# Mixture-of-experts stage of a two-layer decoder: two-pass products for experts with up to 64 tokens, experts ordered on the chip, wide splits in the weight ring, layer loop unrolled

## The reference

```python
def swiglu(h, w1, w3, w2):
    return (jax.nn.silu(h @ w1) * (h @ w3)) @ w2

def moe_swiglu(h, router, w1, w3, w2):
    logits = (h @ router).astype(F32)
    top_v, top_i = lax.top_k(logits, TOP_K)
    gates = jax.nn.softmax(top_v, axis=-1)
    dense_gate = jnp.sum(jax.nn.one_hot(top_i, N_EXPERTS, dtype=F32) * gates[..., None], axis=-2)
    y = jnp.zeros(h.shape, F32)
    for e in range(N_EXPERTS):
        y = y + swiglu(h, w1[e], w3[e], w2[e]).astype(F32) * dense_gate[..., e:e + 1]
    return y.astype(h.dtype)
```

## Time and profile before

| | |
|---|---|
| Median of 3 runs | 1658.33 us (1656.91 to 1659.19) |
| Profiled execution, its own time | 1656.95 us |
| Its span, first to last instruction | 1655.3 us |
| PE busy | 1579.4 us, 95% |
| DVE busy | 1181.1 us, 71% |
| ACT busy | 1001.2 us, 60% |
| Mean granted TensorE clock | 0.977 |
| DMA | 433.46 MB, mean 262 GB/s |
| of it expert weights | 168 DMAs of 2 MB |
| Chain that ended last | PE 90%, DVE 3%, ACT 3%, issue 2%, DMA 1% |

### The profile page before, as it was taken

One profiled execution on the slowest core, in us unless ns is written; L12 is line 12 of the kernel. 1 busy time (PEld: TensorE's weight loads), 2 busy tenths in 40 slices (PEclk: granted clock), 3 DMA queues, 4 the chain that ended last, 5 costly groups with the idle time before them and its releaser, 6 DMA issues.

```text
span 1655.3 us, 21928 instructions
## 1 busy us (share of the span) xinstructions
PE 1579.4 (95%) x7746; PEld 1288.8 (78%) x7746; DVE 1181.1 (71%) x1486; ACT 1001.2 (60%) x1182; POOL 51.8 (3%) x64
## 2 busy tenths in 40 slices
PE   5999989999799978999999999999999999999997
PEld 4776679998676556888888888888888888888885
DVE  1514255555244237998998998998998998998996
ACT  2322254433223134887887887887887887887885
POOL 0230000000032000000000000000000000000000
PEclk9999999999799997999999999999999999999999
DMA  8523415542722182999999999999999999999970
GB/s 297 180 77 126 166 38 193 197 146 61 269 76 77 63 319 102 354 371 339 355 370 334 356 371 331 355 372 331 357 369 333 355 367 335 357 373 329 356 291 25
DMA packets 190711, 433.46 MB, mean 262 GB/s; under 512 B 5679, under 2 KB 30277, under 8 KB 190661
## 3 DMA queue, kind: packets, MB, share of 16 engines
q1 hardware_dynamic: 190468, 432.24, 72.4%
q0 software_dynamic: 192, 0.53, 0.1%
HBM read 431.70 MB, written 1.05 MB: 261 GB/s over the span
## 4 chain that ended last, share of the span: by engine, by line
PE 90%; DVE 3%; ACT 3%; issue 2%; DMA 1%; SPq 0%; ACTq 0%; DVEq 0%; PEldq 0%
PE bank L1216 65%; PE bank L1193 7%; PE bank L1198 5%; PE bank L1474 3%; PE bank L1564 2%; PE bank L1183 2%; PE bank L1615 1%; PE bank L1514 1%; PE bank L1369 1%; DVE w_lo L1150 1%; ACT w_hi L722 1%; PE bank L1581 0%; ACT xg_hi L688 0%; PE bank L1582 0%; ACT r L639 0%
## 5 line engine op out<-in xcount | busy, mean ns | idle before, releaser
L1150 DVE TENSOR_TENSOR w_lo<-ring,w_hi 128x1024 fp32r<-128x1024 f32 x672 | 804.8, 1223 | 90.2 <-ACT w_hi L722 64.9
L722 ACT ACTIVATE w_hi<-ring 128x1024 fp32r<-128x1024 f32 x672 | 709.5, 1062 | 192.0 <-PE bank L1216 188.4
L1216 PE MATMUL bank<-w_hi,xg_hi 128*128 128x512 f32 x896 | 357.3, 399 | 6.9 <-DVE w_lo L1150 6.8
L1216 PE MATMUL bank<-w_lo,xg_hi 128*128 128x512 f32 x896 | 350.4, 391 | 0.0
L1216 PE MATMUL bank<-w_hi,xg_lo 128*128 128x512 f32 x896 | 349.7, 390 | 0.0
L1216 PEld LDWEIGHTS bank<-w_hi,xg_hi 128*128 128x128 f32 x896 | 168.5, 188 | 50.0 <-DVE w_lo L1150 16.7
L1216 PEld LDWEIGHTS bank<-w_lo,xg_hi 128*128 128x128 f32 x896 | 168.5, 188 | 36.6
L1216 PEld LDWEIGHTS bank<-w_hi,xg_lo 128*128 128x128 f32 x896 | 168.9, 188 | 32.6
L1216 PE MATMUL bank<-w_hi,at_hi 128*128 128x512 f32 x448 | 175.9, 393 | 0.0
L1216 PE MATMUL bank<-w_lo,at_hi 128*128 128x512 f32 x448 | 174.5, 389 | 0.0
L1216 PE MATMUL bank<-w_hi,at_lo 128*128 128x512 f32 x448 | 174.4, 389 | 0.0
(11 more groups left out here) (298 smaller groups left out, 1591.4 us busy)
## 6 DMA issues: line engine op xcount, KB each, us to landing
ring<-in_moe_w SPq DMA_DIRECT2D x168, 2048.0 KB, 7.9
ring<-in_ffn_w SPq DMA_DIRECT2D x18, 1536.0 KB, 6.7
ring<-in_w_in SPq DMA_DIRECT2D x6, 2048.0 KB, 14.7
ring<-in_w_out SPq DMA_DIRECT2D x8, 1024.0 KB, 4.9
ring<-in_ffn_w SPq DMA_DIRECT2D x3, 2048.0 KB, 7.8
ring<-in_w_in SPq DMA_DIRECT2D x4, 1024.0 KB, 16.4
ring<-in_xa_wkv SPq DMA_DIRECT2D x2, 2048.0 KB, 12.5
ring<-in_w_in SPq DMA_DIRECT2D x2, 1184.0 KB, 5.6
```

Of the source, the lines that this page charges most:

```text
L722: act.activation(w_hi[:, i % NB, :], ring[:, slot_of(u), PIECE * q:PIECE * q + PIECE], ACT.Copy)\
L1150: dve.tensor_tensor(w_lo[:, i % NB, :], ring[:, slot_of(u), PIECE * q:PIECE * q + PIECE], w_hi[:, i % NB, :], sub).then_inc(S["lo_ready"], 1)
L1216: ins = mm(dst, x, y, start=opens and n % 3 == 0, stop=closes and n % 3 == 2)
```

## The change

**Jobs ordered on the chip.** The table of jobs is built differently. For expert e, a full job is made if its count is above a limit, -1 for expert 0 and 64 for the others (the table `limit`), a second full job if it is above 128, and a small job otherwise. Full jobs come first, then the small ones. The table now also holds each job's expert (SP reads it for every job after the first), the number of full jobs, and a third row of token positions, in which a small job's are shifted by 64. The mask of job 0 is made before the table.

**Small jobs.** The mask of a small job has its up to 64 tokens twice, in columns 0 to 63 and 64 to 127. So `xg_both`, the 128 columns from 64 to 191 of `xg`, is the hi of the tokens beside their lo, and two products, with w_lo and w_hi, do what three did: the rows 0 to 63 of the bank hold hi·(w_hi + w_lo), rows 64 to 127 lo·(w_hi + w_lo). ACT copies both banks out as they are, PE adds the two halves while it transposes them (`fold`, 8 plain float32 matmuls of 64 columns), ACT makes Silu of 256 elements, DVE the product, its hi and its lo side by side in `at_hi`. Both kinds of jobs have a loop of their own on PE, ACT and DVE.

**Wide pieces in place.** A piece is 2048 columns, but for units (1,0) and (3,0), which are cut into 1024, 1024 and 2048: 44 pieces a job. `w_hi` has 4 buffers of 2048. There is no `w_lo` any more: DVE writes it over the weights in the ring slot (`ring_lo`), and PE gives the slot back at the last but one matmul of the unit. `after(unit)` is the unit's last piece plus 3 (`LEAD`). The dense feed-forward keeps pieces of 1024.

**Layers unrolled.** The loop over the two layers is written out on all engines, `If` blocks are decided at build time, and waits are on constants.

```diff
-PIECE, NB = 1024, 4
-QP = 4096 // PIECE
+PIECE, NB = 2048, 4
+FPIECE = 1024
+SMALL = 64
+LEAD = 3
+CUTS = [(u, *cut) for u in range(len(JOB_UNITS))
+        for cut in (((0, 1024), (1024, 2048), (2048, 4096)) if u < 2 else ((0, 2048), (2048, 4096)))]
+LAST = {u: i for i, (u, _, _) in enumerate(CUTS)}
 def after(unit):
-    return QP * UNIT_OF[unit] + QP - 1 + NB
+    return LAST[UNIT_OF[unit]] + LEAD
+    put("limit", np.concatenate(([-1.0], np.full(N_EXP - 1, SMALL), np.full(N_EXP, P)))[None, :])
...
-        w_hi, w_lo = over("w_hi", [P, NB, PIECE]), over("w_lo", [P, NB, PIECE])
-        xg_hi, xg_lo = over("xg_hi", [P, KT, P]), over("xg_lo", [P, KT, P])
+        w_hi = over("w_hi", [P, NB, PIECE])
+        xg = over("xg", [P, KT, 2 * P])
+        xg_hi, xg_lo = xg[:, :, 0:P], xg[:, :, P:2 * P]
+        fold = diag[:, 0, 0:SMALL]
+        xg_both = xg[:, :, SMALL:SMALL + P]
...
-            with sp.Fori(0, DEPTH) as layer:
+            for layer in range(DEPTH):
...
-            with sp.Fori(0, N_EXP) as j:
-                job_loads(j, j)
+            job_loads(0, 0)
             sp.wait_ge(S["jobs_ready"], 1)
...
+            with sp.Fori(1, n_jobs) as j:
+                e = sp.value_load(tabi[0:1, bass.ds(j + 2, 1)], min_val=0, max_val=N_EXP - 1)
+                job_loads(j, e)
```

ACT's pieces (`first_rows` waits for `j_h1` and makes Silu, or a plain copy in a small job; `small_silu` waits for `j_tps`):

```diff
                 for i in range(JOB_PIECES):
-                    if i in (NB - 1, NB):
-                        yrow_out(j, i - (NB - 1))
+                    if i == NB - 1:
+                        for half in range(2):
+                            yrow_out(j, half)
                     for c in range(NCH):
+                        last = i == JOB_PIECES - 1 if c == NCH - 1 else i == after((1, c + 1)) + 1
+                        if not small and i == after((1, c)):
+                            first_rows(c)
+                        if last and small:
+                            small_silu(c)
+                        elif last:
                             transposed(cn[c])
+                        if small and i == after((1, c)) + 1:
+                            first_rows(c)
+                        if small and i == after((3, c)):
+                            act.wait_ge(S["j_h3"], cn[c])
+                            act.activation(s_rows[1], ps[2 * (c % 2) + 1][:, :], ACT.Copy).then_inc(S["j_a"], 1)
```

DVE:

```diff
+                def small_act(c):
+                    dve.wait_ge(S["j_s"], cn[c])
+                    dve.tensor_tensor(s_act, v3(s_sil, 0, 256, 4), v3(ps[4], 256, 512, 4), mult).then_inc(S["j_m"], 1)
+                    dve.wait_ge(S["j_m"], cn[c])
+                    dve.tensor_copy(at_hi[:, :, 0:SMALL], s_act).then_inc(S["j_th"], 1)
+                    dve.wait_ge(S["j_th"], cn[c])
+                    dve.tensor_tensor(at_hi[:, :, SMALL:P], s_act, at_hi[:, :, 0:SMALL], sub).then_inc(S["j_t"], 1)
...
-                    dve.tensor_tensor(w_lo[:, i % NB, :], ring[:, slot_of(u), PIECE * q:PIECE * q + PIECE],
-                                      w_hi[:, i % NB, :], sub).then_inc(S["lo_ready"], 1)
+                    dve.tensor_tensor(ring_lo[slot_of(u)][:, cols], ring[:, slot_of(u), cols],
+                                      w_hi[:, i % NB, 0:cols.stop - cols.start], sub).then_inc(S["lo_ready"], 1)
+            with dve.Fori(0, n_full) as j:
+                job(j, False)
+            with dve.Fori(n_full, n_jobs) as j:
+                job(j, True)
```

PE:

```diff
+                            steps.append((dst[:, :], xh, wh, opens, False))
+                            if small:
+                                steps.insert(len(steps) - 1, (dst[:, :], xh, wl, opens, False))
+                                steps[-1] = (dst[:, :], xh, wh, False, closes)
+                            else:
+                                steps += [(dst[:, :], xh, wl, False, False), (dst[:, :], xl, wh, False, closes)]
+                        for x, (dst, st_, mv, opens, closes) in enumerate(steps):
+                            ins = mm(dst, st_, mv, start=opens, stop=closes, skip_group_check=small)
+                            if x == 0:
+                                ins.then_inc(S["piece_free"], 1)
+                            elif i == LAST[u] and x == len(steps) - 2:
+                                ins.then_inc(slot_free[slot_of(u)], 1)
...
+                    if small:
+                        for x in range(2):
+                            for f in range(4):
+                                i = mm(ps[4][:, 256 * x + SMALL * f:256 * x + SMALL * f + SMALL],
+                                       s_rows[x][:, P * f:P * f + P], fold, start=True, stop=True)
```

## The result

| | kernel before | kernel after |
|---|---|---|
| median of the runs | 1658.76 us (1656.91 to 1659.44) | **1574.15 us** (1573.18 to 1575.1, 4 runs) |
| ratio, 95% interval | | 0.9492 [0.9475, 0.9508] |
| profiled span, granted clock | 1655.3 us | 1571.5 us, 0.975 |

The kernel is 84.6 us faster, 5.1%. 1585 was predicted, with 1558 to 1628 as the range. The medians of the kernel before, measured beside the experiments, lie between 1655.6 and 1657.7 us.

What follows compares the result with a forecast made beforehand. PE was taken to bound the expert stage, with DMA and DVE close behind. Six small jobs -70.4, two full jobs +5.2, unrolled layers -8.3 and the job table +0.5 make -73.0 us: 1585 us, range 1558 to 1628.

Steps and rivals of the forecast that it cites:

- The limit of a small job: Each small job: DVE's work of 107.8 us plus waits of 1.5 and 3.5 paces it at 113 us.
- The DMA floor: Loads of the six small jobs: 5.38 us a unit, 656 us in all, hidden under 678 with 22 to spare.
- rival B: Expert stage: waits overlap, six small jobs take the DMA's 656 us, full jobs lose nothing; 1558 us, chance 0.12.
- The full job: Each of two full jobs: PE's wait at its start, less the turn's gap, adds 2.6 us, making 127.3.
- PE stands 3.3 us: Start of a full job: PE waits 3.3 us for ACT's table load, Silu and wide copy, and DVE's split.
- Unrolled layers: The two layers: issue gaps of 5.44 and 3.85 us go in straight code, -8.3 us; bounds 0 and -12.
- Wide pieces: DVE's splits in a small job: 92.9 us with wide pieces where 95.3 stood, saving 2.4 us only.
- rival C: Expert stage: waits cost more with wide pieces, small jobs 118 us, full jobs +10; 1630 us, chance 0.20.
- D: Small jobs: memory at 352 GB/s is the limit, 727 us for the six; 1634 us, chance 0.05.
- E: Small jobs: short gaps after pieces bring PE to 1.2 GHz, 184 us a job; slower, 2011 us, chance 0.04.
- F: Expert stage: the change doesn't do what it says and all jobs run full; 1671 us, chance 0.01.
- PE still ends last: Small jobs: a sign that the forecast is wrong, PE rather than DVE finishing last; no size given.

Runs made afterwards that it cites:

- late Silu: Kernel after with ACT's first Silu of a full job one piece later (before piece 6, not 5): 1565.96 us, ratio 0.9453.
- late Silu again: The same edit to the kernel after (first Silu of a full job one piece later), measured once more in another call: 1563.47 us, ratio 0.9447.

## Why the prediction was right, and where it was off

**The limit of a small job: right.** DVE paces it and the DMA lies just above. Predicted were 113 us from DVE 107.8, 1.5 and 3.5 of waits. Measured are 107.0 busy, stands of 0.17 to 0.19 us at the chunks rather than 0.25, and 2.9 us at the job's end (1.87 + 0.59 + 0.41): 111.2 with handshakes. A wide split lasts 2.285 us and starts 2.20 after the last (2.30 and 2.21 predicted), a wide copy 1.91 (2.0), the fold 1.70 (1.6). Six jobs at 1.8 us less are 10.7 us, which looks like the prediction's whole miss of 11 us. That the sum is off by no more is luck in part: the full jobs came out 4.0 us dearer than predicted and the start of the stage 3.5 us earlier, which nearly cancel. The working of the 0.25 us has a slip too: 2.05 + 0.6 + 1.9 are 4.55, not 4.65, and give a stand of 0.15, nearer to what was measured.

**The DMA floor: the mechanism right, the margin too large.** 22 us to spare were counted, with 5.38 us for a unit and a job of 113. At 394 GB/s a unit takes 5.32. The run with less work on DVE reached 657.9 us for six jobs, where the floor of rival B was 656, so of the 667.4 us that they take in the kernel after only 9.5 lie above that run. The rule in the Trainium skill, "DMA: Bandwidth & Descriptors", Specifications, of about 358 GB/s, which would have made 1622, doesn't hold for this one core: 392 to 397 GB/s in each of the fifteen slices before the last.

**The full job: size and composition off.** "PE stands 3.3 us": it stood 2.0 us and lost 0.3 more beside it, because the table load was counted in the path and lies inside ACT's wait. Not foreseen were the 1.5 us at 1.2 GHz behind that stand, and 2.7 us from matmuls further apart (0.2331 for 0.2275), the largest term of all. With the 0.5 us of the turn's gap they make 124.7 + 2.3 + 1.5 + 2.7 - 0.5 = 130.7; 130.6 was measured, 127.3 predicted. The first full job rose by 3.3 only (126.3 to 129.6). Together +9.2 where +5.2 was predicted.

**Unrolled layers: right in kind, too small.** 8.3 less 0.5 was predicted, 11.3 (629.0 for 640.3) is in the trace, near the bound of 12. The router's matmuls behind the second gap took 7.0 us and take 5.81.

**Wide pieces: a reason that the prediction misread.** It credited them with 2.4 us a job from fixed costs. DVE's busy time bears that out (2.3 us), the job gains 1.4, and what counts is the 7.1 us that the pieces further ahead are worth, with their buffers. The prediction had this effect in rival C with the sign turned round: it feared that a wait costs more of a wide piece, and the runs show that three wide pieces ahead cover the waits that three narrow ones don't.

**The rivals.** C (1630) and D (1634) are refuted by the lengths of the jobs; E by a granted clock of 1.00 throughout the small jobs, while PE was busy for 103 of 111 us; F by the jobs themselves. F's price of 1671 for eight full jobs was too low: with seven and one small job 1664.55 was measured, and an eighth full one would add 18.5, 1683 by this estimate. B came closest, by its small jobs (111.2 against 109.3), but the full jobs did lose. Of the signs of being wrong, "PE still ends last" isn't met, but it isn't far off: in the chain of a small job PE has 36% and DVE 32%, and most of the 24% of issue stands beside a running split.

**The sum in the traces:** -11.3 (start of the stage) + 3.3 + 5.9 (full jobs) - 6 x 13.5 = -83 us; the last update of `hotT` moved from 1639.8 to 1556.6, 83.2.

## What to carry to other kernels

When an engine meets waits at fixed points of its order, ask how many columns of work the next engine still has in hand, not how many pieces: narrow pieces six ahead, with seven buffers, did what wide ones three ahead did, and narrow ones three ahead lost 49 us. Before a loop that uses an activation table, look in the trace for ACT_TABLE_LOAD inside the loop: one tiny activation ahead of it, in idle time, took two loads out of every turn, 6.9 us by the medians. When PE's work of a stage is cut, work out the DMA's floor from a deep-queue stretch first, since it tells how much of the cut can be had.

## What was not expected of the hardware

- A stand of PE of 2.02 us in a stretch that had been at full clock was followed by 3.4 us at 1.2 GHz, which cost another 1.5 us. In the run with seven full jobs the same stand came in each of them, and the fall in every second one only.
- 512-column matmuls of the same shape start 0.2275 us apart in before, and in the full jobs of the experiments 0.2285 with narrow pieces and `lo` in its own buffer, 0.2317 with `lo` in the ring, 0.2320 there with six pieces ahead, 0.2318 to 0.2330 with wide pieces. The place of `lo` explains the larger part and the order of products some 0.001; why a place or an order should matter stays open.
- The stage begins between 620.0 and 630.2 us in kernels that differ little or not at all ahead of it (620.0 and 624.8 in two executions of one kernel). It goes with the granted TensorE clock of the first 600 us, the third number from the right:

```profile
0.00:600.00 600.00, 560.13 (x3031) 448.98 (x3032) 246.62 (x504) 187.60 (x326) 51.81 (x64) 0.96 0.44 153
0.00:600.00 600.00, 558.45 (x3043) 448.41 (x3044) 248.78 (x510) 190.75 (x331) 51.94 (x64) 0.97 0.45 155
0.00:600.00 600.00, 557.12 (x3070) 446.45 (x3070) 251.63 (x516) 193.08 (x336) 51.82 (x64) 0.98 0.45 158
```

(the kernel after, late Silu, late Silu again; their stages begin at 629.0, 624.8 and 620.0 us). In all twelve unrolled traces a clock of 0.96 goes with 627.3 to 630.2, 0.97 with 624.8 to 626.0 and 0.98 with 620.0 to 622.3. So the medians scatter by more than most edits change the stage, and the jobs were compared by their own lengths. Why the clock fell less often in some executions stays open.
